# How the SwiGLU product is turned for the down projection: 128x128 squares on the matrix engine, or 32x32 squares and moves

## The chip, the cores and the metric

One core of a Trainium2 chip runs the whole program. The metric is the device time of one execution in microseconds (us). The core has the matrix engine PE (TensorE), the vector engine DVE, the scalar engine ACT, the engine POOL (GpSimd) and SP (SyncE), which here issues transfers. The engines are ordered among themselves by semaphores. 16 DMA engines carry the transfers.

## The reference, cut to what matters

```python
def swiglu(h, w_in, w_out):          # h: 256 x 2048, w_in: 2048 x 11264, w_out: 5632 x 2048, all float32
    gu = h @ w_in
    gate, up = gu[..., :D_FF], gu[..., D_FF:]
    return (jax.nn.silu(gate) * up) @ w_out

h = h + 0.5 * swiglu(rmsnorm(h, ffn1_norm), ffn1_w_in, ffn1_w_out)
# ... a pooling and gated-linear-attention mixer, and its output projection ...
h = h + 0.5 * swiglu(rmsnorm(h, ffn2_norm), ffn2_w_in, ffn2_w_out)
# ... then two attention layers (second_block), which the change doesn't touch
```

The sequence has 256 tokens, which lie on the partitions as 2 tiles of 128. The product silu(gate) * up has 5632 columns; these are the dimension that the second matmul sums over, so the product has to be turned before it can be an operand of it.

## The kernel before, in words

The kernel is a row of stages. A stage is n rounds; a round makes 512 output columns for both token tiles from 2048 rows of weights, which come in 8 chunks of 256 rows. Every float32 number is used as a sum of a rounded part (hi) and a rest (lo), so each product takes three matmuls: hi by hi, hi by lo, lo by hi (L1273 to L1275). A chunk is 2 row tiles by 2 token tiles by 3 matmuls, 12 matmuls of 128x512.

Each engine runs its own program over the same stages. A round of an ffn_in or ffn_out stage is as follows.

- **SP** (`load`) waits for each chunk c of round k until its place in `raw` is free, which is when chunk c of round k-1 has been split (`lo_done`), and issues two transfers for it. So SP is 8 chunks ahead of the split.
- **ACT** (`split_hi`, L1337) rounds a chunk into `whi`, and **DVE** (`split_lo`, L1522) subtracts to get `wlo`. There are 4 places for split chunks (`SPLIT`), so a chunk is split as soon as PE is through with the chunk 4 before it.
- **PE** multiplies the 8 chunks of the round.
- In the order of ACT and DVE a round k is: split chunks 4 to 7 of round k, turn what there is to turn (`batches_of`), split chunks 0 to 3 of round k+1 (`first_half`), and then `evacuate` round k. Chunk 3 of round k+1 can be split when PE has finished round k.

The two feed-forward networks have 3 ffn_in stages each, of 8, 8 and 6 rounds, each followed by an ffn_out stage of 4 rounds that uses what the ffn_in stage has made. An ffn_in round makes 256 columns of gate and the 256 matching columns of up. `evacuate` has ACT take silu of the gate half (L1390), and DVE multiply it by the up half into `hid[:, u]` (L1557; u is the parity of the round). That block of 256 tokens by 256 columns is then a batch `("hid", k)`: in the next round, between chunks 3 and 4, PE transposes it in 4 squares of 128x128 into a PSUM bank (`transposes`, L1231), ACT rounds the bank into the operand of the next stage (`operand_hi`, L1357), and DVE subtracts to get its rest (`operand_lo`, L1533). The block of an ffn_in stage's last round is a `Batch` of the ffn_out stage and is turned in its round 0. An ffn_out stage multiplies by block c in its chunk c; before each chunk of round 0 PE waits for the batch that makes the operand (`s.need[c]`).

First rounds are written out, the others are loops of two rounds (`paired_rounds`), whose waits count in registers. `tm` is a work area of 2 x 2048 numbers per partition that `hid` overlays.

Of the kernel before, what the change touches and what calls it, by code (L numbers as in the profile page):

```python
# [33 lines left out]
P = 128  # L34
# [5 lines left out]
NB = 512  # L40
HB = NB // 2
CH = 8
SPLIT = 4
# [83 lines left out]
def build(nc, A, out, upto=None):  # L127
    ctx = ExitStack()
    with ctx:
# [35 lines left out]
        h = sb("h", [P, TT, D])  # L165
        at = overlaid([("tm", [P, TT, D], F32)], [("hid", [P, 2, TT, HB], F32)])
        tm, hid = at["tm"], at["hid"]
        ab = overlaid([("bc", [P, 2, D], F32)],
# [91 lines left out]
        for n, s in enumerate(stages):  # L260
# [19 lines left out]
            if s.kind == "ffn_in" and nxt:  # L280

                s.hid_pair = nxt.pair
                nxt.before.setdefault(0, []).append(Batch(((s.n - 1) % 2,), nxt.pair, 2 * (s.n - 1)))
            if s.name in follows and nxt:
# [5 lines left out]

        n, latest = 0, {}
        for s in stages:
            for b in s.ahead:
                b.number, latest[b.pair, b.kt], n = n, n, n + 1
            for k in range(s.n):
                for c in range(CH):
                    if k == 0:
                        for b in s.mid.get(c, []):
                            b.number, latest[b.pair, b.kt], n = n, n, n + 1
                    if c == 4:  # L300
                        for b in s.before.get(k, []):
                            b.number, latest[b.pair, b.kt], n = n, n, n + 1
                        if s.kind == "ffn_in" and k:
                            if k == 1:
                                s.hid_batch0 = n
                            latest[s.hid_pair, 2 * (k - 1)], n = n, n + 1
                    if k == 0:
                        s.need[c] = latest[s.pair, s.chunk_tiles(c)[-1] // 2 * 2] + 1

        def batches_of(s, k, peeled):  # L310

            got = list(s.before.get(k, [])) if peeled else []
            if s.kind == "ffn_in" and not (peeled and k == 0):
                got.append(("hid", k))
            return got

        def resolve(s, b, u):

            if isinstance(b, Batch):
                return b.number, b.number % 2, b.pair, b.kt, b.gain  # L320
            k = b[1]
            return k - 1 + s.hid_batch0, (u - 1 + s.hid_batch0) % 2, s.hid_pair, (k - 1) * 2, None

# [84 lines left out]
        t_full, t_hi, t_done = sem("transposed"), sem("operand_hi_done"), sem("operand_done")  # L408
        silu_done = sem("silu_done")
        ident_in, const_in = sem("ident_in"), sem("const_in")  # L410


        LO0, USED0, FREE0 = CH, SPLIT, 2

# [717 lines left out]
        def _(sp):  # L1132
            xv = A["x"].rearrange("a (t p) n -> p (a t) n", p=P)
            for s in stages:
                w, k0, n0 = s.weights

                def load(k, u):
                    for c in range(CH):
# [10 lines left out]
                        for i in range(2):  # L1149
# [6 lines left out]
                            else:  # L1156
                                src = w[lo:lo + P, bass.ds(col + i * HB, HB)]
                                dst = raw[:, c, 0, i * HB:(i + 1) * HB]
                            sp.dma_start(dst, src).then_inc(landed[c], 16)

                paired_rounds(sp, s, load)
# [45 lines left out]
        def _(pe):  # L1207
            pe.sem_inc(chunk_used, USED0)

            def transposes(s, b, u):  # L1210
                number, parity, pair, kt, gain = resolve(s, b, u)
                dst = bank[4 + parity]
                if isinstance(b, Batch):
                    issued[0] = number + 1
                if not isinstance(b, Batch) or number >= 2:

                    pe.wait_ge(t_done, number - 1)
                if emitted[4 + parity]:

                    pe.wait_ge(freed_s[4 + parity], emitted[4 + parity])  # L1220
                if isinstance(b, tuple):

                    pe.wait_ge(acc_free, s.a0 + b[1] + FREE0)
                    src = [hid[:, (u - 1) % 2, t, j * P:(j + 1) * P] for j in range(2) for t in range(TT)]
                elif isinstance(b.source, tuple):
                    pe.wait_ge(acc_free, s.a0 + FREE0)
                    src = [hid[:, b.source[0], t, j * P:(j + 1) * P] for j in range(2) for t in range(TT)]
                else:
                    src = b.source(kt)
                for n, piece in enumerate(src):  # L1230
                    ins = pe.transpose(dst[:, n * P:(n + 1) * P], piece, ident)  # L1231
                ins.then_inc(t_full, 1)
# [52 lines left out]
            for s in stages:  # L1285
# [4 lines left out]
                def round_(k, u):  # L1290
# [6 lines left out]
                    for c in range(CH):  # L1297
# [28 lines left out]
        def _(act):  # L1326
# [14 lines left out]
            def operand_hi(s, b, u):  # L1341
                number, parity, pair, kt, gain = resolve(s, b, u)
                act.wait_ge(t_full, number + 1)
# [113 lines left out]
            for n, s in enumerate(stages):  # L1457
                nxt = stages[n + 1] if n + 1 < len(stages) else None

                def second_half(k, u):  # L1460
# [45 lines left out]
        def _(dve):  # L1506
            dve.sem_inc(lo_done, LO0)
            dve.sem_inc(acc_free, FREE0)
            steps = sem("vector_step")
            stepped = [0]  # L1510
# [14 lines left out]
            def operand_lo(s, b, u):  # L1525
                number, parity, pair, kt, gain = resolve(s, b, u)
                dve.wait_ge(t_hi, number + 1)
# [115 lines left out]
            for n, s in enumerate(stages):  # L1643
# [4 lines left out]
                def round_(k, u):  # L1648
# [61 lines left out]
```

## Time and profile before

| | us |
|---|---|
| median of 3 runs | 2788.77 |
| lowest and highest | 2787.61, 2790.61 |
| the profiled execution, its own time | 2788.64 |
| its span, first to last instruction | 2786.8 |
| PE busy | 2750.0 (99%) |
| DVE busy | 1495.4 (54%) |
| ACT busy | 1289.3 (46%) |
| DMA queue q1, share of 16 engines | 57.3% |
| mean granted PE clock | 0.998 |

The span is what the profile's views divide up; the execution's own time is 1.84 us longer. "Busy" counts the time an instruction is at work. PE's matmuls overlap, so its busy time is not its work at peak. The chain of waits follows the work back from the last instruction to what released each step.

### The profile page before, as it was taken

The numbers are of one execution on the slowest core, as the hardware profiler recorded it, in microseconds if no ns is written. First come the engines' busy times: TensorE is split into PE (matmuls) and PEld (weight loads), VectorE is DVE, ScalarE is ACT, GpSimd is POOL, SyncE is SP. The second block draws the span as 40 slices with busy tenths as digits, with TensorE's granted clock in tenths as the row PEclk, the third lists the DMA queues.
The fourth block names the chain that finished last, engine by engine and source line by source line (L and its number), as shares of the span: only waits on it lengthen the run. The fifth ranks groups of instructions, "written<-read, shape, count | busy, mean of one in ns | idle before, by whom it ended". The sixth has DMA issues, their size and how long they took to land.

```text
span 2786.8 us, 34415 instructions
## 1 busy us (share of the span) xinstructions
PE 2750.0 (99%) x12534; PEld 2260.5 (81%) x12534; DVE 1495.4 (54%) x1705; ACT 1289.3 (46%) x1653; POOL 63.6 (2%) x72
## 2 busy tenths in 40 slices
PE   7999999999999999999999999999999999999998
PEld 6888888888888788888888888887888888777877
DVE  4555455554544455455455545558555576455566
ACT  5443444344544455443444344544554464554463
POOL 1000000000000000000000000020000000020000
PEclk9999999999999999999999999999999999999999
DMA  9666666665644465655665565654465565546663
GB/s 258 191 189 193 191 190 187 195 189 177 193 153 151 147 199 183 189 191 193 190 189 190 193 189 174 196 183 152 136 204 169 171 196 188 157 137 198 185 177 131
DMA packets 375511, 506.09 MB, mean 182 GB/s; under 512 B 36022, under 2 KB 228736, under 8 KB 374608
## 3 DMA queue, kind: packets, MB, share of 16 engines
q1 hardware_dynamic: 373376, 495.84, 57.3%
q0 software_dynamic: 1824, 8.37, 0.9%
q8 instruction: 85, 1.39, 0.2%
q14 instruction: 50, 0.41, 0.0%
q10 hardware_dynamic: 176, 0.07, 0.0%
HBM read 502.06 MB, written 2.10 MB: 181 GB/s over the span
## 4 chain that ended last, share of the span: by engine, by line
PE 95%; DVE 2%; POOL 1%; ACT 1%; DMA 1%; issue 0%; SPq 0%; ACTq 0%; DVEq 0%; POOLq 0%
PE bank L1273 30%; PE bank L1275 30%; PE bank L1274 30%; PE bank L1231 2%; DMA h<-in_x_dram 1%; DVE wlo L1522 1%; POOL rope_b L850 1%; PE bank L997 0%; PE bank L798 0%; PE bank L782 0%; PE bank L1014 0%; PE bank L1023 0%; ACT whi L1337 0%; DVE isc L907 0%; PE bank L489 0%
## 5 line engine op out<-in xcount | busy, mean ns | idle before, releaser
L1522 DVE TENSOR_TENSOR wlo<-raw,whi 128x1024 fp32r<-128x1024 f32 (+2 forms) x976 | 1154.3, 1187 | 1227.6 <-ACT whi L1337 1223.6
L1337 ACT CAST whi<-raw 128x1024 fp32r<-128x1024 f32 (+2 forms) x976 | 988.6, 1016 | 1369.1 <-PE bank L1275 1363.3
L1273 PE MATMUL bank<-whi,p_hi 128*128 128x512 f32 x2016 | 799.1, 396 | 2.7 <-DVE wlo L1522 2.7
L1275 PE MATMUL bank<-whi,p_lo 128*128 128x512 f32 x2016 | 786.9, 390 | 0.0
L1274 PE MATMUL bank<-wlo,p_hi 128*128 128x512 f32 x2016 | 786.7, 390 | 0.0
L1273 PE MATMUL bank<-whi,q_hi 128*128 128x512 f32 x1696 | 667.9, 394 | 1.6 <-DVE wlo L1522 1.6
L1275 PE MATMUL bank<-whi,q_lo 128*128 128x512 f32 x1696 | 661.1, 390 | 0.0
L1274 PE MATMUL bank<-wlo,q_hi 128*128 128x512 f32 x1696 | 660.4, 389 | 0.0
L1273 PEld LDWEIGHTS bank<-whi,p_hi 128*128 128x128 f32 x2016 | 379.8, 188 | 86.6 <-issue 10.0
L1274 PEld LDWEIGHTS bank<-wlo,p_hi 128*128 128x128 f32 x2016 | 379.8, 188 | 79.8 <-issue 3.1
L1275 PEld LDWEIGHTS bank<-whi,p_lo 128*128 128x128 f32 x2016 | 379.5, 188 | 80.2
L1273 PEld LDWEIGHTS bank<-whi,q_hi 128*128 128x128 f32 x1696 | 318.7, 188 | 68.4 <-issue 3.9
L1275 PEld LDWEIGHTS bank<-whi,q_lo 128*128 128x128 f32 x1696 | 318.4, 188 | 67.1
L1274 PEld LDWEIGHTS bank<-wlo,q_hi 128*128 128x128 f32 x1696 | 318.9, 188 | 64.3
L1231 PE MATMUL bank<-con,h 128*128 128x128 f32 x224 | 32.5, 284 | 13.1 <-DMA h<-in_x_dram 9.3
L1231 PEld LDWEIGHTS bank<-con,h 128*128 128x128 f32 x224 | 27.4, 146 | 19.4 <-issue 12.2
L1557 DVE SCALAR_TENSOR_TENSOR hid<-bank,small,sg 128x256 f32<-128x256 f32 x88 | 38.3, 476 | 4.1 <-ACT sg L1390 4.1
L1390 ACT ACTIVATE sg<-bank,small 128x256 f32<-128x256 f32 x88 | 36.7, 468 | 0.0
L1568 DVE SCALAR_TENSOR_TENSOR h<-bank,h 128x512 f32<-128x512 f32 x56 | 35.9, 682 | 0.0
L1373 ACT ACTIVATE sg<-h 128x512 f32<-128x512 f32 x32 | 19.9, 624 | 29.9 <-DVE h L1568 29.9
L1538 DVE SCALAR_TENSOR_TENSOR p_lo<-bank,vec,p_hi 128x256 fp32r<-128x256 f32 x40 | 16.9, 477 | 21.5 <-ACT p_hi L1361 21.3
L1361 ACT ACTIVATE p_hi<-bank,vec 128x256 fp32r<-128x256 f32 x40 | 16.1, 473 | 25.5 <-PE bank L1231 25.5
(260 smaller groups left out, 998.8 us busy)
## 6 DMA issues: line engine op xcount, KB each, us to landing
raw<-in_ffn_w_in_dram SPq DMA_DIRECT2D x704, 256.0 KB, 2.9
raw<-in_ffn_w_out_dram SPq DMA_DIRECT2D x320, 256.0 KB, 3.0
raw<-in_w_in_a_dram SPq DMA_DIRECT2D x192, 256.0 KB, 3.0
raw<-in_w_in_mix_dram SPq DMA_DIRECT2D x128, 256.0 KB, 3.1
raw<-in_w_ple_gate_dram SPq DMA_DIRECT2D x128, 256.0 KB, 3.6
raw<-in_w_in_b_dram SPq DMA_DIRECT2D x128, 256.0 KB, 3.1
raw<-in_w_out_mix_dram SPq DMA_DIRECT2D x64, 256.0 KB, 3.2
raw<-in_w_o_a_dram SPq DMA_DIRECT2D x64, 256.0 KB, 3.4
```

The costliest lines, as they stand in the source:

```text
L850: ins = eng.tensor_tensor(dst, x, f, ALU.mult)
L1231: ins = pe.transpose(dst[:, n * P:(n + 1) * P], piece, ident)
L1273: pe.matmul(o, xht, wh, start=(kt == t_first), stop=False)
L1274: pe.matmul(o, xht, wl, start=False, stop=False)
L1275: ins = pe.matmul(o, xlt, wh, start=False, stop=(kt == t_last))
L1337: act.copy(whi[:, c % SPLIT, 0:n, 0:w], raw[:, c, 0:n, 0:w]).then_inc(hi_done, 1)
L1373: ins = act.activation(sgw[:, t, :], h[:, t, blk * NB:(blk + 1) * NB], ACT.Square, accum_out=parts[:, t, blk:blk + 1])
L1390: ins = act.activation(sg[:, u, t, :], pair[t][:, 0:HB], ACT.Silu, scale=rstd[:, t:t + 1])
L1522: dve.tensor_tensor(wlo[:, c % SPLIT, 0:n, 0:w], raw[:, c, 0:n, 0:w], whi[:, c % SPLIT, 0:n, 0:w].bitcast(F32), ALU.subtract).then_inc(lo_ ...
L1538: ins = dve.scalar_tensor_tensor(lo_[:, kt + j, :], src[:, j * SEQ:(j + 1) * SEQ], vec[:, g:g + 1], hi_[:, kt + j, :].bitcast(F32), ALU.mu ...
L1557: ins = dve.scalar_tensor_tensor(hid[:, u, t, :], pair[t][:, HB:NB], rstd[:, t:t + 1], sg[:, u, t, :], ALU.mult, ALU.mult)
L1568: ins = dve.scalar_tensor_tensor(hb, pair[t][:, :], c, hb, ALU.mult, ALU.add)
```

## The change

In place of ACT and DVE waiting for PE's squares, each block takes another way. DVE, straight after it has written `hid[:, u]`, transposes it with two instructions that turn each 32x32 square in itself (`hidq`). SP then moves the squares to their places with 16 transfers from SBUF to SBUF, each of 32 partitions by 128 numbers (`hidf`). ACT rounds from `hidf` into the operand, and DVE subtracts. A block of round k is turned at the end of round k, moved by SP while it loads round k+2 (after chunk 3), and rounded and subtracted by ACT and DVE after the splits of chunks 4 to 7 of round k+1. The last block of each ffn_in stage is also turned by DVE but not moved; PE transposes it from `hid` in round 0 of ffn_out as before.

```diff
-        at = overlaid([("tm", [P, TT, D], F32)], [("hid", [P, 2, TT, HB], F32)])
+        at = overlaid([("tm", [P, TT, D], F32)], [("hid", [P, 2, TT, HB], F32), ("hidq", [P, 2, 4, 2, TT, QB], F32),
+                                               ("hidf", [P, 2, 4, 2, TT, QB], F32)])
...
         def batches_of(s, k, peeled):
-            got = list(s.before.get(k, [])) if peeled else []
-            if s.kind == "ffn_in" and not (peeled and k == 0):
-                got.append(("hid", k))
-            return got
+            return list(s.before.get(k, [])) if peeled else []
+
+        def hidden_behind(s, k, u, peeled, behind):
+            if s.kind == "ffn_in" and not (peeled and k < behind):
+                return s, k - behind, (u - behind) % 2
+            if s.kind == "ffn_out" and peeled and k < behind - 1:
+                return s.hid_of, s.hid_of.n - behind + k, (s.hid_of.n - behind + k) % 2
+            return None
+
+        def moved_by(s, k, u):
+            return 16 * 16 * (s.moved0[u] + 1) + 8 * 16 * (k - u)
...
         @block.sync
+            def move_hidden(s, k, u):
+                sp.wait_ge(hid_turned, s.turned0 + k + 1)
+                sp.wait_ge(hid_done, s.turned0 + k - 1 + HID0)
+                for q in range(4):
+                    for f in range(4):
+                        sp.dma_start(hidf[f * QB:(f + 1) * QB, u, q, :, :, :], hidq[q * QB:(q + 1) * QB, u, f, :, :, :]).then_inc(hid_moved[u], 16)
...
                             sp.dma_start(dst, src).then_inc(landed[c], 16)
+                        if c == 3:
+                            made = hidden_behind(s, k, u, isinstance(k, int), 2)
+                            if made:
+                                move_hidden(*made)
...
         @block.tensor
-                if isinstance(b, tuple):
-                    pe.wait_ge(acc_free, s.a0 + b[1] + FREE0)
-                    src = [hid[:, (u - 1) % 2, t, j * P:(j + 1) * P] for j in range(2) for t in range(TT)]
...
-                            pe.wait_ge(t_done, s.need[c])
+                            if s.kind == "ffn_out" and s.chunk_tiles(c)[-1] // 2 == s.hid_of.n - 1:
+                                pe.wait_ge(t_done, s.last_hid.number + 1)
+                            elif s.kind == "ffn_out":
+                                pe.wait_ge(hid_done, s.hid_of.turned0 + s.chunk_tiles(c)[-1] // 2 + 1 + HID0)
+                            else:
+                                pe.wait_ge(t_done, s.need[c])
...
         @block.scalar
+            def hidden_hi(s, k, u):
+                act.wait_ge(hid_moved[u], moved_by(s, k, u))
+                for j in range(2):
+                    ins = act.copy(pair_hi[s.hid_pair][:, k * 2 + j, :].rearrange("p (t q n) -> p t q n", t=TT, q=4),
+                                   hidf[:, u, :, j, :, :].rearrange("p q t n -> p t q n"))
+                ins.then_inc(hid_hi, 1)
...
                     for b in batches_of(s, k, peeled):
                         operand_hi(s, b, u)
+                    made = hidden_behind(s, k, u, peeled, 1)
+                    if made:
+                        hidden_hi(*made)
...
         @block.vector
+            def hidden_lo(s, k, u):
+                dve.wait_ge(hid_hi, s.hid0 + k + 1)
+                for j in range(2):
+                    hi_, lo_ = (pair[s.hid_pair][:, k * 2 + j, :].rearrange("p (t q n) -> p t q n", t=TT, q=4)
+                                for pair in (pair_hi, pair_lo))
+                    ins = dve.tensor_tensor(lo_, hidf[:, u, :, j, :, :].rearrange("p q t n -> p t q n"), hi_.bitcast(F32), ALU.subtract)
+                ins.then_inc(hid_done, 1)
...
                                                        sg[:, u, t, :], ALU.mult, ALU.mult)
                     ins.then_inc(acc_free, 1)
+                    dve.wait_ge(acc_free, at_ + FREE0)
+                    for t in range(TT):
+                        ins = dve.transpose(hidq[:, u, :, :, t, :].rearrange("p f j n -> p j f n"),
+                                            hid[:, u, t, :].rearrange("p (j f n) -> p j f n", j=2, f=4))
+                    ins.then_inc(hid_turned, 1)
...
                     for b in batches_of(s, k, peeled):
                         operand_lo(s, b, u)
+                        if s.kind == "ffn_out" and b is s.last_hid:
+                            dve.sem_inc(hid_done, 1)
+                    made = hidden_behind(s, k, u, peeled, 1)
+                    if made:
+                        hidden_lo(*made)
```

## Rows read from the trace of the kernel before

**Rows 1.** The page, its first part (engines) and fourth (chain, by engine).
```profile
PE 2750.0 (99%) x12534; PEld 2260.5 (81%) x12534; DVE 1495.4 (54%) x1705; ACT 1289.3 (46%) x1653; POOL 63.6 (2%) x72
...
PE 95%; DVE 2%; POOL 1%; ACT 1%; DMA 1%; issue 0%; SPq 0%; ACTq 0%; DVEq 0%; POOLq 0%
```

**Rows 2.** Groups with shapes apart, whole span; columns as on the page.
```profile
L1273 PE MATMUL bank<-whi,p_hi 128*128 128x512 f32 x2016 | 799.1, 396 | 2.7 <-DVE wlo L1522 2.7
...
L1231 PE MATMUL bank<-con,hid 128*128 128x128 f32 x176 | 26.3, 271 | 0.0
```

**Rows 3.** Chain in order of time, 346 to 350 us: start, us, what.
```profile
346.49 0.23 PE bank L1275
346.72 0.44 PE bank L1231 x4
347.15 0.23 PE bank L1273
```

**Rows 4.** Timeline of ACT, 336 to 371 us: start, us, what, idle before it.
```profile
336.88 0.83 ACT L1390 ACTIVATE sg<-bank,small 128x256 f32<-128x256 f32 x2
...
344.03 1.05 ACT L1337 CAST whi<-raw 128x1024 fp32r<-128x1024 f32 x1 [1.67 <-PE bank L1275]
346.75 1.05 ACT L1337 CAST whi<-raw 128x1024 fp32r<-128x1024 f32 x1 [1.67 <-PE bank L1275]
347.71 0.58 ACT L1357 CAST q_hi<-bank 128x512 f32 x1
349.96 1.05 ACT L1337 CAST whi<-raw 128x1024 fp32r<-128x1024 f32 x1 [1.67 <-PE bank L1275]
...
369.96 0.58 ACT L1357 CAST q_hi<-bank 128x512 f32 x1
```

**Rows 5.** Timeline of DVE, 337 to 341 us.
```profile
338.15 0.87 DVE L1557 SCALAR_TENSOR_TENSOR hid<-bank,small,sg 128x256 f32<-128x256 f32 x2
```

**Rows 6.** SP: timeline at 346 us, weight issues at 783 to 806 us, their landing.
```profile
346.51 0.93 SPq L1159 DMA_DIRECT2D raw<-in_ffn_w_in_dram  x2
...
L1159 SPq DMA_DIRECT2D raw<-in_w_in_mix_dram x22: 327/431/902, 783.4 to 805.9; - x22
...
raw<-in_w_in_mix_dram SPq DMA_DIRECT2D x10, 8.0 KB, 1.7
```

**Rows 7.** DMA: packets at 783 to 797 us, queue q1 there and on the page, window 305 to 350.
```profile
DMA packets 1513, 0.24 MB, mean 17 GB/s; under 512 B 1440, under 2 KB 1440, under 8 KB 1512
...
q1 hardware_dynamic: 1512, 0.23, 10.3%
...
q1 hardware_dynamic: 373376, 495.84, 57.3%
...
305.00:350.00 45.00, 45.00 (x204) 37.21 (x204) 22.49 (x23) 19.29 (x23) 0.00 (x0) 1.00 0.61 190
```

**Rows 8.** Start of ffn1_in0, timelines of DVE and PE, 54 to 60 us.
```profile
54.94 0.88 DVE L1557 SCALAR_TENSOR_TENSOR hid<-bank,small,sg 128x256 f32<-128x256 f32 x2 [2.06 <-ACT sg L1390]
...
57.62 4.62 DVE L1522 TENSOR_TENSOR wlo<-raw,whi 128x1024 fp32r<-128x1024 f32 x4
...
59.34 0.60 PE L1231 MATMUL bank<-con,hid 128*128 128x128 f32 x4
```

**Rows 9.** Start of ffn2_in0, timelines of DVE and ACT, 1101 to 1110 us.
```profile
1102.03 0.88 DVE L1557 SCALAR_TENSOR_TENSOR hid<-bank,small,sg 128x256 f32<-128x256 f32 x2 [2.06 <-ACT sg L1390]
...
1108.90 0.58 ACT L1357 CAST p_hi<-bank 128x512 fp32r<-128x512 f32 x1
```

**Rows 10.** Groups with shapes apart: prices by size.
```profile
L1522 DVE TENSOR_TENSOR wlo<-raw,whi 128x1024 fp32r<-128x1024 f32 x912 | 1116.8, 1229 | 1145.2 <-ACT whi L1337 1141.3
L1337 ACT CAST whi<-raw 128x1024 fp32r<-128x1024 f32 x912 | 955.2, 1050 | 1292.2 <-PE bank L1275 1288.1 <-DMA raw<-in_ffn_w_in_dram 2.5 <-PE bank L1270 0.8
...
L1522 DVE TENSOR_TENSOR wlo<-raw,whi 128x512 fp32r<-128x512 f32 x48 | 32.8, 689 | 63.0 <-ACT whi L1337 63.0
...
L1337 ACT CAST whi<-raw 128x512 fp32r<-128x512 f32 x48 | 29.5, 618 | 57.5 <-PE bank L1275 57.2
```

More of the change, by code:

```diff
@@ L41 @@
 HB = NB // 2
+QB = 32
 CH = 8
@@ L165, in build @@
         h = sb("h", [P, TT, D])
-        at = overlaid([("tm", [P, TT, D], F32)], [("hid", [P, 2, TT, HB], F32)])
-        tm, hid = at["tm"], at["hid"]
+        at = overlaid([("tm", [P, TT, D], F32)], [("hid", [P, 2, TT, HB], F32), ("hidq", [P, 2, 4, 2, TT, QB], F32),
+                                               ("hidf", [P, 2, 4, 2, TT, QB], F32)])
+        tm, hid, hidq, hidf = at["tm"], at["hid"], at["hidq"], at["hidf"]
         ab = overlaid([("bc", [P, 2, D], F32)],
@@ L280, in build @@
             if s.kind == "ffn_in" and nxt:
-                s.hid_pair = nxt.pair
-                nxt.before.setdefault(0, []).append(Batch(((s.n - 1) % 2,), nxt.pair, 2 * (s.n - 1)))
+                s.hid_pair, nxt.hid_of = nxt.pair, s
+                nxt.last_hid = Batch(lambda kt, u=(s.n - 1) % 2: [hid[:, u, t, j * P:(j + 1) * P] for j in range(2) for t in range(TT)],
+                                     nxt.pair, 2 * (s.n - 1))
+                nxt.before.setdefault(0, []).append(nxt.last_hid)
             if s.name in follows and nxt:
@@ L289, in build @@
                         Batch(columns(h), pair, 4 * k + 2 * j, GAIN[gain] if gain else None) for j in range(2))
-        n, latest = 0, {}
+        n, turns, hids, moves, latest = 0, 0, 0, [0, 0], {}
         for s in stages:
@@ L294, in build @@
                 b.number, latest[b.pair, b.kt], n = n, n, n + 1
+            if s.kind == "ffn_in":
+                s.turned0, s.hid0, s.moved0 = turns, hids, list(moves)
+                turns, hids = turns + s.n, hids + s.n - 1
+                moves = [moves[0] + s.n // 2, moves[1] + s.n // 2 - 1]
             for k in range(s.n):
@@ L302, in build @@
                             b.number, latest[b.pair, b.kt], n = n, n, n + 1
[L303 to L307, printed above, removed]
+                    if k == 0 and s.kind != "ffn_out":
                         s.need[c] = latest[s.pair, s.chunk_tiles(c)[-1] // 2 * 2] + 1
         def batches_of(s, k, peeled):
-            got = list(s.before.get(k, [])) if peeled else []
-            if s.kind == "ffn_in" and not (peeled and k == 0):
-                got.append(("hid", k))
-            return got
[L317 to L322, printed above, removed]
+            return list(s.before.get(k, [])) if peeled else []
[7 more added lines that the diff above has]
+            return 16 * 16 * (s.moved0[u] + 1) + 8 * 16 * (k - u)
         def acc(a, t):
@@ L409, in build @@
         silu_done = sem("silu_done")
+        hid_turned, hid_hi, hid_done = sem("hidden_turned"), sem("hidden_hi_done"), sem("hidden_done")
+        hid_moved = [sem(f"hidden_moved_{u}") for u in range(2)]
         ident_in, const_in = sem("ident_in"), sem("const_in")
-        LO0, USED0, FREE0 = CH, SPLIT, 2
+        LO0, USED0, FREE0, HID0 = CH, SPLIT, 2, 2
         def round_before(s, k):
@@ L1210, in transposes @@
             def transposes(s, b, u):
-                number, parity, pair, kt, gain = resolve(s, b, u)
+                number, parity, pair, kt, gain = b.number, b.number % 2, b.pair, b.kt, b.gain
                 dst = bank[4 + parity]
-                if isinstance(b, Batch):
-                    issued[0] = number + 1
-                if not isinstance(b, Batch) or number >= 2:
+                issued[0] = number + 1
+                if number >= 2:
                     pe.wait_ge(t_done, number - 1)
@@ L1220, in transposes @@
                     pe.wait_ge(freed_s[4 + parity], emitted[4 + parity])
-                if isinstance(b, tuple):
-                    pe.wait_ge(acc_free, s.a0 + b[1] + FREE0)
-                    src = [hid[:, (u - 1) % 2, t, j * P:(j + 1) * P] for j in range(2) for t in range(TT)]
[L1225 to L1230, printed above, removed]
+                for n, piece in enumerate(b.source(kt)):
                     ins = pe.transpose(dst[:, n * P:(n + 1) * P], piece, ident)
@@ L1341, in operand_hi @@
             def operand_hi(s, b, u):
-                number, parity, pair, kt, gain = resolve(s, b, u)
+                number, parity, pair, kt, gain = b.number, b.number % 2, b.pair, b.kt, b.gain
                 act.wait_ge(t_full, number + 1)
@@ L1508, in _ @@
             dve.sem_inc(acc_free, FREE0)
+            dve.sem_inc(hid_done, HID0)
             steps = sem("vector_step")
@@ L1525, in operand_lo @@
             def operand_lo(s, b, u):
-                number, parity, pair, kt, gain = resolve(s, b, u)
+                number, parity, pair, kt, gain = b.number, b.number % 2, b.pair, b.kt, b.gain
                 dve.wait_ge(t_hi, number + 1)
```

## The prediction

> **What bounds the kernel now.** I read the page's first part, then its chain: PE is busy 99% of the span and the chain that ended last is PE for 95% of it [rows 1]. Then I read the groups with shapes apart. The reader is to see that the matmuls wait for almost nothing: 2.7 us of idle time before one of the two large matmul groups, all of it on DVE's split weights, and none at all before the transposes of `hid` [rows 2]. ACT and DVE, on the other hand, do nothing for more than half of the time: ACT has 1.67 us free before each split, and it is PE that ends this wait [rows 4]. So time comes off only where PE has less to do, and anything that ACT, DVE, SP and the DMA engines get in exchange costs nothing as long as split weights are ready when PE comes to them.
>
> **What PE loses.** The six ffn_in stages have 8, 8, 6, 8, 8 and 6 rounds, 44 blocks, and 44 x 4 = 176 transposes, which the group confirms [rows 2]. The last block of each stage stays, so 38 batches of 4 transposes go. The price of a batch has three readings. The group gives a mean of 271 ns for one, but 26.3 us for 176, since they overlap [rows 2]; 4 of these are 0.60. The chain, which counts each step only until the next begins, gives 0.44 us for the four [rows 3]. And the cadence of ACT, which here is set by PE, shows what a batch does to PE's chunks: a split follows the one before it by 2.72 us (344.03 to 346.75), but by 3.21 us where the batch lies between (346.75 to 349.96), which is 0.49 more; and a round is 369.96 - 347.71 = 22.25 us, where 8 chunks of 2.72 would be 21.76, again 0.49 [rows 4]. What the cadence has above the chain, 0.05, I put down to a slower start of the matmuls behind the transposes. I take 0.48 us between the two and nearer to the cadence, as it is measured from end to end. 38 x 0.48 = 18.2 us; the ends are 38 x 0.44 = 16.7 and 38 x 0.49 = 18.6. The waits that go with the batches on PE (for `t_done`, `acc_free`) had no idle time, so they give nothing more.
>
> The Trainium skill prices such a transpose otherwise. TensorE: Matmul & The Clock Gate, section Part 4: PE-mode transpose, has about 390 ns in isolation and about 275 ns in a kernel for 128x128 in bf16. By that, 152 transposes would be an estimated 42 us; the trace agrees with the 275 as the length of one (271 ns) but not as its cost, since four overlap into 0.44.
>
> **What DVE gets.** 88 square transposes of 128x256, 2 per block. The trace has no such instruction. Subtracts of 1024 and 512 columns take 1229 and 689 ns [rows 10], so one of 256 would take 689 - 540/2 = 419; the multiply of 128x256 takes 476 with an advance of 0.40 when two follow each other [rows 5]. I take 0.42 each, 0.85 for both with the wait between; below it could be next to nothing, above as long as the 1024-column subtract, 1.23 each. `hidden_lo` is 2 x 0.42 for a removed 0.68 of 512 columns (the 512-column price above). The room is ample: 8 splits of 1.23 and these make some 12.5 us in a round of 22.
>
> **What ACT gets.** Two copies of 256 columns for one of 0.58 [rows 4]. Casts of 1024 and 512 columns take 1050 and 618 ns [rows 10], so 256 are about 400, 0.80 for both. The short runs of 32 numbers in their addresses could double that; 1.6 still fits in the 1.67 free before a split [rows 4].
>
> **What SP gets, and the new wait.** 38 x 16 = 608 transfers, and ahead of each 16 a wait for DVE's squares. Two weight transfers of 256 KB are issued in 0.93 us; transfers of 8 KB in the narrow stage are issued in 327 to 902 ns, median 431 [rows 6]. So the issue doesn't depend on the size, and 16 of them take 16 x 0.37 = 5.9 to 16 x 0.47 = 7.5 us; I take 7.5. An 8 KB transfer lands after 1.7 us [rows 6].
>
> Now the times, in the round of [rows 4] and [rows 5]. DVE has written `hid` at 338.15 + 0.87 = 339.0 and the squares at 339.9. SP has by then issued chunk 3 of its load and waits; it issues until 347.4, and the last move lands at 349.1, or a microsecond later if the weights ahead of it in the queue hold it. ACT comes to `hidden_hi` where L1357 is now, 347.7, and waits some 1.4 to 2.6 us. Behind ACT's wait stand the splits of the next round's chunks 0 to 3, behind them DVE's. PE needs the first of these when it starts the next round: four chunks after its batch place, 346.7 + 4 x 2.72 = 357.6. Split hi and lo take 1.05 + 1.23 = 2.3, the two copies 0.8, so the last move may land at 354.5 without PE noticing. That is 4 us or more to spare, and the lag is made up at 1.67 us per chunk. It would be gone if an issue took (354.5 - 1.7 - 339.9) / 16 = 0.81 us.
>
> Behind SP's wait stand the weight transfers of chunks 4 to 7 of the round after next. They are issued up to 7 us late. Their cover is a full round of 22 us, so 15 are left for a landing that takes 1.7 us at 8 KB, and ACT doesn't wait for them. The moves don't pass POOL's queue.
>
> The DMA engines are 0.61 busy in such a round [rows 7]. A block adds 16 x 32 packets of 512 B, and from 10 transfers of 128 rows making 1440 packets I read 16 more per transfer for the semaphore: 768. At 15 ns each (10.3% of 16 engines for 14 us, over 1512 packets) this is 0.7 us per engine, at 68 ns (57.3% of the span over 373376) it is 3.3 [rows 7]. The share becomes 0.64 to 0.76, so weights keep landing in time.
>
> The Trainium skill, DMA: Bandwidth & Descriptors, section Measured (HBM→SBUF, 128 partitions, SWDGE, issued from GpSimd), says that transfers under 64 KB are dominated by descriptors, and its section Anatomy of one DMA — SWDGE (gpsimd) path puts a fixed cost of about 2.0 us on each. If those 2.0 us were paid one after another, 16 moves would be an estimated 32 us and wouldn't fit in a round.
>
> **Two late starts.** In ffn1_in0 the first `hid` is late, at 55.8 us, since the first silu waited for the norm [rows 8]. DVE's split of chunk 4 of round 1, the first of the four in its row, ends at 58.8 now; with 0.85 us of squares ahead of it, 59.7, and PE wants it at 59.3 [rows 8]: 0.4 us lost. The move of that block: squares at 56.7, issued until 64.2, landed at 65.9 to 67.1; the bound there is 59.3 + 10.9 - 3.1 = 67.1. So nothing is lost, but with hardly any room, and up to 2 us could be. In ffn2_in0 `hid` is ready at 1102.9 and the squares at 1103.8, landed at 1113.0; L1357 begins at 1108.9, which is 1.0 behind the batch place, so the bound is 1107.9 + 10.9 - 3.1 = 1115.7 [rows 9]: hidden. The other four stages start like the round above. The ffn_out stages lose nothing: block n-2 is done in ACT's and DVE's round n-1 of ffn_in, at least a whole round ahead of its chunk, and the last block goes as before.
>
> **Sum.** -18.2 + 0.4 = -17.8. The profiled execution's span of 2786.8 becomes 2769.0, its own time of 2788.64 becomes 2770.8, and the median, 0.13 above that, 2771.0. Its own range, from the ends of the terms: 16.7 - 2.4 = 14.3 to 18.6, 2770 to 2774.5, and 1 us each side for the runs.
>
> **Rivals.**
>
> *Moves land late (slower).* The place is ACT's wait in `hidden_hi`; it decides from 0.81 us per issue. For it speaks that SP does have issues of 0.90 us among the small transfers [rows 6]. At 0.90 each plus a gap of 0.04, 16 take 15.0 us, 2.1 beyond the 12.9 that there is, in each of 38 blocks: +80 - 18 = +62, about 2851. Against it: the median is 0.43, and only few are that long. Were moves served one after another at 1.7 us each, they would take 27.2 us where 14.6 are there: 38 x 12.6 - 18 = +461, about 3250. Against that speaks that two weight transfers are issued within 0.93 us, less than the landing of even an 8 KB one [rows 6]. 6% for both.
>
> *The gain is eaten, no change.* This takes 12 us or more back: 0.32 us per block, from matmuls that run slower beside the SBUF traffic, from a stall of 2 us in each of the first rounds (6 x 2 = 12), or because the squares take DVE far longer than any row suggests. 2777 to 2787, say 2783. Every stage would have to start as late as ffn1_in0, and four of the six don't. 6%. A smaller loss of 3 to 10 us by the same ways, 2775 to 2782: 12%.
>
> *PE's transposes cost their full length.* 152 x 0.271 = 41.2 us, 2747. Against it are the chain's 0.44 for four and the cadence. 2%. The Trainium skill's price named above would give the same.
>
> *The change doesn't take the work off PE*, if PE waits in ffn_out for `hid_done` as long as it saved. All blocks but the last are done before, so 1%, and it would be no change.
>
> *The forecast*, 2771: 73%.
>
> About 0.2% or 5.6 us is what a measurement of this kernel can tell from no change. Faster: 73 + 2 + nearly all of the 12, 87%. Same: 7%. Slower: 6%. The range goes from 2767 to 2781; most of what it leaves out is on the slow side.
>
> **What would show it.** In the changed profile L1231 on `hid` has 24 instructions; the cast behind the old batch place follows its predecessor by 2.72 us and not 3.21 unless ACT waits for the moves, and a round takes 21.8 us. SP shows rows of 16 transfers in 6 to 7.5 us. ACT's wait for hidf's transfer is 1 to 3 us in each block. The square transposes take about 0.4 us. The idle time of L1273 behind DVE stays under 5 us; if it is tens of microseconds, the first rival holds. If the round shrinks by 0.44 or less, my price of the batch was too high.

## The result

| | before | after |
|---|---|---|
| median, us | 2789.69 (4 runs) | 2772.55 (4 runs) |
| lowest and highest | 2787.61, 2790.94 | 2770.90, 2772.59 |
| span of the profiled execution | 2786.8 | 2769.1 |

The ratio is 0.9935 with a 95% interval of 0.9921 to 0.9949: 17.1 us faster by the medians, 2771.0 was forecast. A second set of five runs, made beside experiment 2, gave 2773.18 and 0.9942 (0.9929 to 0.9956), 16.1 us faster than the kernel before beside it (2789.25).

The page after, first and fourth part. They answer to [rows 1].

```profile
PE 2731.3 (99%) x12382; PEld 2244.7 (81%) x12382; DVE 1527.7 (55%) x1831; ACT 1290.0 (47%) x1691; POOL 63.6 (2%) x72
...
PE 95%; DVE 2%; ACT 1%; POOL 1%; DMA 1%; SPq 1%; issue 0%; ACTq 0%; DVEq 0%; POOLq 0%
```

PE is still 99% of the span and 95% of the chain. It has 152 instructions fewer (12382 for 12534), DVE has 126 more and ACT 38 more.

Groups with shapes apart, answering to [rows 2], and the source line of the moves with its landing time. Columns of the last two: instructions with shortest, median and longest duration in ns, and us to landing.

```profile
L1284 PE MATMUL bank<-whi,p_hi 128*128 128x512 f32 x2016 | 797.4, 396 | 4.0 <-DVE wlo L1550 4.0
...
L1242 PE MATMUL bank<-con,hid x24: 270/272/273, 213.7 to 1731.3; 128*128 128x128 f32 x24
...
L1149 SPq DMA_DIRECT2D hidf<-hidq x608: 507/590/1437, 56.7 to 1711.9; - x152
...
DMA to landing us min/median/max: 1.7/1.8/5.6
```

24 of the 176 transposes of `hid` are left, as forecast. PE's idle time behind DVE's split went from 2.7 to 4.0 us in this group. A move takes SP 590 ns to issue, and 16 come at one per 0.63 us, where I had 0.37 to 0.47 from weights.

Timeline of ACT after, two rounds, answering to [rows 4].

```profile
344.89 1.05 ACT L1353 CAST whi<-raw 128x1024 fp32r<-128x1024 f32 x1 [1.67 <-PE bank L1286]
349.35 0.71 ACT L1384 CAST q_hi<-hidf 128x256 f32 x2 [3.40 <-DMA hidf<-hidq]
349.97 2.00 ACT L1353 CAST whi<-raw 128x1024 fp32r<-128x1024 f32 x2
353.06 1.05 ACT L1353 CAST whi<-raw 128x1024 fp32r<-128x1024 f32 x1 [1.08 <-PE bank L1286]
...
366.65 1.05 ACT L1353 CAST whi<-raw 128x1024 fp32r<-128x1024 f32 x1 [1.67 <-PE bank L1286]
371.06 0.71 ACT L1384 CAST q_hi<-hidf 128x256 f32 x2 [3.35 <-DMA hidf<-hidq]
```

ACT stands still for 3.40 us until the last move has landed, then makes up for it: two casts run together, the next one still finds 1.08 us of idle time ended by PE. From one pair of copies to the next is 371.06 - 349.35 = 21.71 us; before, it was 22.25 [rows 4]. The next four rounds take 21.74 to 21.77, so the round lost 0.5 us, and PE never noticed ACT's wait.

Timeline of DVE and of SP in the same rounds, answering to [rows 5, 6].

```profile
358.00 0.87 DVE L1594 SCALAR_TENSOR_TENSOR hid<-bank,small,sg 128x256 f32<-128x256 f32 x2
358.91 0.77 DVE L1599 STREAM_TRANSPOSE hidq<-hid 128x256 f32<-128x256 f32 x2
```

```profile
338.00 10.04 SPq L1149 DMA_DIRECT2D hidf<-hidq  x16
348.28 10.94 SPq L1176 DMA_DIRECT2D raw<-in_ffn_w_in_dram  x16
359.71 10.04 SPq L1149 DMA_DIRECT2D hidf<-hidq  x16
```

The two square transposes take 0.77 us together. SP begins at once (359.71, the squares being there at 359.68) and needs 10.04 us for 16. The 16 moves and the 16 weight transfers of a round fill 10.04 + 10.94 of 21.7 us, which no step of the forecast had looked at.

### The profile page after: what moved, and what is told of

The parts are those of the page before. It is cut to its first block, busy times and chain, and to the rows that moved or that the text cites. A ratio compares the mean times of both kernels' runs of the same rounds, so it can differ in the third digit from the quotient of the medians.

```text
span 2769.1 us, 34994 instructions
## 1 busy us (share of the span) xinstructions
PE 2731.3 (99%) x12382; PEld 2244.7 (81%) x12382; DVE 1527.7 (55%) x1831; ACT 1290.0 (47%) x1691; POOL 63.6 (2%) x72
## 3 DMA queue, kind: packets, MB, share of 16 engines
q1 hardware_dynamic: 402560, 505.84, 58.3%
## 4 chain that ended last, share of the span: by engine, by line
PE 95%; DVE 2%; ACT 1%; POOL 1%; DMA 1%; SPq 1%; issue 0%; ACTq 0%; DVEq 0%; POOLq 0%
PE bank L1284 30%; PE bank L1286 30%; PE bank L1285 30%; PE bank L1242 1%; DMA h<-in_x_dram 1%; DVE wlo L1550 1%; POOL rope_b L858 1%; PE bank L1005 0%; PE bank L806 0%; ACT whi L1353 0%; PE bank L790 0%; PE bank L1022 0%; PE bank L1031 0%; SPq L1149 0%; DVE isc L915 0%
## 5 line engine op out<-in xcount | busy, mean ns | idle before, releaser
L1576 DVE TENSOR_TENSOR q_lo<-hidf,q_hi 128x256 f32 (+1 forms) x38 | 14.5, 422 | 64.7 <-ACT q_hi L1384 64.7
L1576 DVE TENSOR_TENSOR p_lo<-hidf,p_hi 128x256 f32 (+1 forms) x38 | 14.5, 422 | 62.7 <-ACT p_hi L1384 62.7
L1384 ACT CAST q_hi<-hidf 128x256 f32 (+1 forms) x38 | 13.6, 404 | 73.2 <-DMA hidf<-hidq 73.2
L1384 ACT CAST p_hi<-hidf 128x256 f32 (+1 forms) x38 | 13.6, 404 | 70.0 <-DMA hidf<-hidq 70.0
```

The source lines that it names most:

```text
L1384: ins = act.copy(pair_hi[s.hid_pair][:, k * 2 + j, :].rearrange("p (t q n) -> p t q n", t=TT, q=4), hidf[:, u, :, j, :, :].rearrange("p q ...
L1576: ins = dve.tensor_tensor(lo_, hidf[:, u, :, j, :, :].rearrange("p q t n -> p t q n"), hi_.bitcast(F32), ALU.subtract)
```

## What the clock adds to the comparison

Windows of 5 us at the three places where PE's clock was below full while it had work before, and, after, at its two and at one of the old ones. (The clock also falls in the last 5 us or so of each span, where PE has nothing left to do; that stretch is left out.) The columns are the window, its length, busy time and count of PE, weight loads, DVE, ACT and POOL, then granted clock, DMA share, GB/s.

```profile
26.00:31.00 5.00, 4.66 (x16) 3.94 (x17) 2.10 (x3) 1.77 (x3) 0.00 (x0) 0.66 1.09 359
842.00:847.00 5.00, 5.00 (x15) 4.03 (x16) 0.00 (x0) 2.94 (x6) 0.00 (x0) 0.66 0.28 100
2091.00:2096.00 5.00, 4.63 (x18) 4.09 (x19) 2.30 (x4) 1.17 (x2) 0.00 (x0) 0.66 0.34 105
```

```profile
28.00:33.00 5.00, 5.00 (x19) 3.89 (x19) 2.33 (x4) 2.00 (x4) 0.00 (x0) 0.69 1.09 359
842.00:847.00 5.00, 5.00 (x27) 4.17 (x26) 3.29 (x4) 2.83 (x5) 0.00 (x0) 1.00 0.57 188
2533.00:2538.00 5.00, 4.78 (x19) 4.22 (x20) 2.15 (x4) 1.17 (x2) 0.00 (x0) 0.66 0.35 105
```

A mean of 0.66 is some 3.4 us at the lower level of 1.2 GHz in a window otherwise at 2.4 GHz. At 842 us PE gets through 15 matmuls before and 27 after in the same 5 us, though not the same ones. By my estimate each such stretch costs what the clock fell short, 5 x 0.34 = 1.7 us. Three before and two after: 2786.8 - 5.1 = 2781.7 against 2769.1 - 3.4 = 2765.7, so by this count the change itself is worth 16.0 us of the 17.7 between the two spans. The same counting (the clock's shortfall, window by window) puts the second profile of the changed kernel at 2772.1 - 6.8 = 2765.3. Below, "at full clock" means a span reduced in this way. It rests on one profile of each kernel. The only measure of its error is that the two profiles of the changed kernel differ by 0.4 us, so a difference of that size isn't shown by it. It is used because the timed runs of one kernel lie further apart than that: of the changed kernel's four, three are within 0.06 us of each other and the fourth is 1.6 lower, about one such stretch.

## The experiments

**1. What four transposes cost PE.** All 44 hid batches of the kernel before, transposed twice over.

```diff
-                for n, piece in enumerate(src):
+                hidden = isinstance(b, tuple) or isinstance(b.source, tuple)
+                for n, piece in list(enumerate(src)) * (2 if hidden else 1):
```

> The kernel before, with each of its 44 hid batches transposed twice over (8 PE transposes into the same bank for 4; the second four write what the first four wrote). My theory: PE takes four further transposes at 0.44 us by the chain of waits, and the slower restart of the matmuls behind a batch, which was 0.05, doesn't double. So 44 x 0.44 = 19.4 us slower, 19 to 21. Rival, transposes cost their full length of 271 ns: 176 x 0.271 = 48 us slower. Rival, a batch costs mostly by its restart and its waits and little by the count of its transposes: under 10 us slower.

Measured: 2807.09 us, ratio 1.0063 (1.0046 to 1.0080), 16.8 us slower by the medians and 2800.8 - 2781.7 = 19.1 at full clock. The chain in order of time, one batch:

```profile
350.73 0.23 PE bank L1276
350.96 0.87 PE bank L1232 x8
351.83 0.23 PE bank L1274
```

Eight transposes pass in 0.87 us, twice the 0.44 of [rows 3]. Four cost 19.1 / 44 = 0.43 us, which is my 0.44, and the rival of 48 us falls. So does the figure of 275 ns that the Trainium skill gives for 128x128 in bf16 (TensorE: Matmul & The Clock Gate, Part 4: PE-mode transpose), taken as a price: it is a length.

**2. Is the new way hidden?** No moves, and ACT waits for the squares only.

```diff
-                        if c == 3:
-                            made = hidden_behind(s, k, u, isinstance(k, int), 2)
-                            if made:
-                                move_hidden(*made)
...
-                act.wait_ge(hid_moved[u], moved_by(s, k, u))
+                act.wait_ge(hid_turned, s.turned0 + k + 1)
```

(and `hidq` for `hidf` in what ACT and DVE read). This kernel leaves the squares where DVE wrote them, so it doesn't compute the same function.

> The changed kernel without any of the 608 moves and without ACT's wait for them: ACT waits for DVE's squares and makes the operand from the unmoved squares, so each feed-forward network works on wrongly placed numbers. My theory: the moves cost nothing except in ffn1_in0, where they make ACT 8.4 us late and PE about 1.8 us idle, so 1.5 to 2.2 us faster than the changed kernel, and PE's idle time behind DVE's split falls from 5.6 + 2.2 to about 6. Rival, the moves or ACT's wait of 3.4 us in each block cost PE a little every time (0.1 us or more per block): 6 us faster or more. Rival, the late start costs nothing and the forecast was off by the clock alone: no difference.

Beside it on the same chip, the changed kernel again:

> The changed kernel unaltered, so that the small differences of the runs beside it can be read on one chip. My theory: 16 to 18.5 us faster than before (38 x 0.48 = 18.2 less 2.0 at the start of ffn1_in0, where PE waits 0.2 and 1.6 us or a little more for split weights), a ratio of 0.9934 to 0.9943. It has no rival of its own; the other three are read against it.

Measured: 2769.41 us against 2773.18, 3.8 us by the medians, whose runs spread over 5.5 and 3.2 us; at full clock 2771.7 - 8.5 = 2763.2 against 2765.3: 2.1 us faster. The view of waits tells where they were (columns: who, for whom, us in total, times, longest). The changed kernel's second profile first, then the one without moves:

```profile
ACT q_hi L1384 <- DMA hidf<-hidq: 74.6, 19, 8.5
...
PE bank L1284 <- DVE wlo L1550: 5.7, 10, 1.3
...
PEld bank L1284 <- DVE wlo L1550: 2.3, 2, 1.7
```

```profile
PE bank L1280 <- DVE wlo L1546: 4.4, 9, 1.0
...
PEld bank L1280 <- DVE wlo L1546: 0.6, 1, 0.6
```

ACT waits for moves for 74.6 us in the 19 blocks of the first network and for 69.9 in those of the second, and all of it is worth 2.1 us at the end. The rival of 0.1 us per block would be 6 us or more faster. The loss is in ffn1_in0: PE and its weight loads wait for DVE's splits for 8.0 us in all against 5.0, and of these 5.2 against 2.2 lie between 40 and 75 us. The same place in the changed kernel's first profile, answering to [rows 8] (timelines of SP, ACT and DVE):

```profile
56.72 11.16 SPq L1149 DMA_DIRECT2D hidf<-hidq  x16
```

```profile
69.09 0.71 ACT L1384 CAST q_hi<-hidf 128x256 fp32r<-128x256 f32 x2 [8.39 <-DMA hidf<-hidq]
```

```profile
58.46 4.62 DVE L1550 TENSOR_TENSOR wlo<-raw,whi 128x1024 fp32r<-128x1024 f32 x4
```

16 moves took 11.16 us there, the last landed at 69.1, 8.39 us after ACT was ready for it, and my bound for it was 67.1. 69.1 - 67.1 = 2.0.

**3. Where does it stop being hidden?** 20, 24 and 32 moves per block; the ones beyond 16 write copies to an unused area.

```diff
-                for q in range(4):
-                    for f in range(4):
-                        sp.dma_start(hidf[f * QB:(f + 1) * QB, u, q, :, :, :], hidq[q * QB:(q + 1) * QB, u, f, :, :, :]).then_inc(hid_moved[u], 16)
+                for m in range(MOVES):
+                    q, f = m % 16 // 4, m % 4
+                    to = hidf if m < 16 else hidx
+                    sp.dma_start(to[f * QB:(f + 1) * QB, u, q, :, :, :], hidq[q * QB:(q + 1) * QB, u, f, :, :, :]).then_inc(hid_moved[u], 16)
```

> The changed kernel with 24 transfers per block for 16; the last 8 write copies of squares to an unused area and add to the same count that ACT waits for. My theory: a move is issued every 0.628 us (16 in 10.04), so 24 take 15.1 us. What PE can hide in a round, by the changed kernel's timeline: PE starts the next round at 366.6 + 10.9 = 377.4, of this 0.71 + 1.05 + 1.23 = 3.0 us are copies and the first split, so the last move may land at 374.4; the squares are there at 359.7 and the last landing takes 1.8, which leaves 12.9 us for the issues. So 15.1 is 2.2 too long, for 38 blocks: 82 us slower than the changed kernel, about 2852 to 2856, and the round takes 23.9 us. Rival, the wait is hidden anyway up to a full round (ACT and DVE catch up): within 5 us of the changed kernel. Rival, the wait for the moves already costs PE time in each block of the changed kernel: then 8 more moves cost their full 5.0 us per block, 190 us slower.

> The same with 32 transfers per block. My theory: 32 x 0.628 = 20.1 us of issues, 7.2 beyond the 12.9, 38 x 7.2 = 274 us slower than the changed kernel, about 3045, and a round of 28.9 us. If SP can't fit 32 moves and 16 weight transfers into that round (20.1 + 16 x 0.47 to 0.68 = 27.6 to 31 us), it is up to 350 slower. Rival, hidden up to a full round: under 30 slower. Rival, each further move costs in full: 38 x 16 x 0.628 = 382 us slower.

Measured: 24 moves 2912.53 us, ratio 1.0441 (1.0424 to 1.0459), 140 us slower than the changed kernel's 2772.55 for 82 expected; 32 moves, a single run, 3116.14, 344 slower for 274 expected. The first lies between my 82 and the rival's 190; for the second I had allowed up to 350 in case SP can't fit its issues into the round. I then tried a second model:

> The changed kernel with 20 transfers per block. 24 and 32 cost 140 and 344 us where I had 82 and 274, so I have a second model of the late case, a cycle. Once ACT is late by more than PE's lead, all four splits of the next round are done one after another ahead of the multiply that makes the next hid block, so from a landing to the next squares it takes 7.9 us (24 moves: ACT's copies at 358.89, squares at 366.80), then 0.65 us per move with its gap, then 1.3 to the copies. A round is 7.9 + 1.3 + 0.65 n: 25 for 24 moves (25.8 measured, 0.6 of it because SP was still at its weights), 30 for 32. For 20 it is 22.2, against PE's own 21.75: 0.45 x 38 = 17 us, so 10 to 25 us slower than the changed kernel, 2783 to 2798. The bound that I worked out first, 12.9 us of issues, is not reached by 20 x 0.628 = 12.6, and would have 0 to 3 us slower.

Measured: 2813.04 us, ratio 1.0081 (1.0064 to 1.0098), 40 us slower. Both models fall. The timelines of SP and DVE with 20 moves show what neither had:

```profile
360.81 10.22 SPq L1178 DMA_DIRECT2D raw<-in_ffn_w_in_dram  x16
371.20 10.06 SPq L1151 DMA_DIRECT2D hidf<-hidq  x16
381.30 2.49 SPq L1151 DMA_DIRECT2D hidx<-hidq  x4
384.06 9.68 SPq L1178 DMA_DIRECT2D raw<-in_ffn_w_in_dram  x16
```

```profile
369.04 0.78 DVE L1601 STREAM_TRANSPOSE hidq<-hid 128x256 f32<-128x256 f32 x2
```

The squares are there at 369.82, but SP is at its weight transfers until 371.03 and begins the moves at 371.20. It has no pause between: 384.06 - 360.81 = 23.25 us from one set of weights to the next, and ACT's copies are 385.10 - 361.88 = 23.22 apart. SP's own work is the round. 16 weight transfers issued without a pause take 9.3 to 10.4, a move 0.63, with some 0.4 between: 20 moves make 22.3 to 23.4, 24 make 25.6 (357.93 to 383.50 in that trace), 32 make 30.2 (464.34 to 494.52, ACT's copies 30.20 apart).

```profile
464.34 9.61 SPq L1178 DMA_DIRECT2D raw<-in_ffn_w_in_dram  x16
474.11 10.02 SPq L1151 DMA_DIRECT2D hidf<-hidq  x16
484.18 10.09 SPq L1151 DMA_DIRECT2D hidx<-hidq  x16
494.52 5.54 SPq L1178 DMA_DIRECT2D raw<-in_ffn_w_in_dram  x9
```

Over all rounds inside the stages that the traces show, ACT's copies are 22.8, 25.3 and 30.5 us apart in the mean, since the weight transfers vary; the round of 23.2 shown is one of the longer ones. For 38 blocks that is 40, 135 and 332 us above 21.75, and 40, 140 and 344 were measured. By the same count 16 moves make 9.8 + 10.04 + 0.4 = 20.2 of 21.75 us. SP is 93% full, and by my estimate two more moves would be as many as fit. I didn't take the rest of the load off SP with the number of moves kept, so that SP alone decides is read from the rows, not isolated by a run.

**4. Why a move takes 0.59 us.** Five series of 16 transfers behind the end of the kernel, each waited for before the next.

```diff
+                sp.dma_start(raw[32:64, c, i, 0:128], raw[0:32, c, i, 0:128]).then_inc(sem("shape_a"), 16)
...
+                sp.dma_start(raw[0:128, c, i, 0:512], win[0:128, n * 128:n * 128 + 512]).then_inc(sem("shape_e"), 16)
```

> The changed kernel with five series of 16 transfers added on SP behind the stored output, each series on a line of its own and waited for before the next: (a) SBUF to SBUF, 32 partitions x 512 B, other partitions; (b) SBUF to SBUF, 128 partitions x 512 B; (c) DRAM to SBUF, 32 x 512 B; (d) DRAM to SBUF, 128 x 512 B; (e) DRAM to SBUF, 128 x 2 KB. The question is why a move is issued every 0.628 us when weight transfers have 0.37 us of issue. My theory: it is the two SBUF ends, so (a) and (b) are at 0.51 to 0.59 us per issue, (c), (d) and (e) at 0.33 to 0.43. Rival, it is the small count of partitions: (a) and (c) slow, (b), (d), (e) fast. Rival, it is the load of the queue in the round: all five at 0.33 to 0.43. The time of the kernel itself means little here: some 50 us longer.

The source lines of the five, in that order:

```profile
L1196 SPq DMA_DIRECT2D raw<-raw x16: 512/590/592, 2770.0 to 2779.4; - x16
...
L1200 SPq DMA_DIRECT2D raw<-raw x16: 519/601/607, 2781.2 to 2790.8; - x16
...
L1204 SPq DMA_DIRECT2D raw<-in_w_in_mix_dram x16: 364/421/425, 2792.8 to 2799.7; - x16
...
L1208 SPq DMA_DIRECT2D raw<-in_w_in_mix_dram x16: 328/432/457, 2801.3 to 2808.6; - x16
...
L1212 SPq DMA_DIRECT2D raw<-in_w_in_mix_dram x16: 328/446/739, 2810.5 to 2818.3; - x16
```

The theory holds, at or a little above the ranges that I gave. With both ends in SBUF an issue takes 590 to 601 ns, from DRAM into SBUF 421 to 446, for 16 KB as for 64 or 256 KB, 32 partitions or 128. So for the issue what counts is the number of transfers and what they join, not what they carry.

**5. Fewer issues: through DRAM.** One transfer out, four back, with a semaphore `hid_out` and a DRAM buffer `away` of their own.

```diff
-                for q in range(4):
-                    for f in range(4):
-                        sp.dma_start(hidf[...], hidq[...]).then_inc(hid_moved[u], 16)
+                sp.dma_start(away[u], hidq[:, u, :, :, :, :].rearrange("p f j t n -> p f (j t n)")).then_inc(hid_out[u], 16)
+                sp.wait_ge(hid_out[u], 16 * (s.moved0[u] + 1) + 8 * (k - u))
+                for f in range(4):
+                    sp.dma_start(hidf[f * QB:(f + 1) * QB, u, :, :, :, :].rearrange("p q j t n -> p q (j t n)"),
+                                 away[u, :, f, :].rearrange("(q i) n -> i q n", q=4)).then_inc(hid_moved[u], 16)
```

> The changed kernel with another way to move the squares: one transfer of all 128 partitions from SBUF to DRAM, a wait for it on SP, and four transfers from DRAM to SBUF, each of 32 partitions by 4 squares: 5 issues for 16. My theory: a write of 256 KB lands after some 2.5 to 4 us, four loads are issued at 0.43 us and the last lands 1.8 us later, so the block is there 6 to 8 us behind DVE's squares, where it now takes 11.9. ACT comes to it 8 us behind the squares, so its wait falls from 3.4 us to under 0.5, in ffn1_in0 from 8.4 to about 3, and PE's 1.8 us of idle time there go. 1.5 to 2 us faster than the changed kernel, the same as without moves. Rival, a round trip through DRAM with a wait between takes longer than 11.9 us: ACT waits longer than now, no gain, and up to 3 us more at the start.

```profile
336.85 0.35 SPq L1149 DMA_DIRECT2D hidden_away<-hidq  x1
340.37 1.76 SPq L1152 DMA_DIRECT2D hidf<-hidden_away  x4
342.38 15.66 SPq L1180 DMA_DIRECT2D raw<-in_ffn_w_in_dram  x16
```

```profile
PE bank L1288 <- DVE wlo L1554: 4.4, 9, 1.0
...
ACT q_hi L1388 <- DMA hidf<-hidden_away: 1.8, 1, 1.8
```

SP's part ends 5.3 us after it began, and ACT's wait is 1.8 us once in place of 144.5 in 38 blocks. The time: median 2773.20 of runs from 2768.49 to 2773.60, ratio 0.9934 (0.9920 to 0.9948), the same as the changed kernel's 2773.18, and at full clock 2771.4 - 6.8 = 2764.6, 0.7 us faster where I had 1.5 to 2. That is too near to the 0.4 between two profiles of one kernel to be a gain shown. The waits for DVE's splits at the start are those of the kernel without moves (2.2 us between 40 and 75 us), so by them the 2.1 us should have come; whether they did stays open.

**6. The last block too.** First the edit in common: `last_hid` and its batch go, and `hidden_behind` serves one round more of ffn_out.

```diff
-            if s.kind == "ffn_out" and peeled and k < behind - 1:
+            if s.kind == "ffn_out" and peeled and k < behind:
```

Through DRAM:

> The kernel of the run before, and the last block of each ffn_in stage takes the same way (in round 0 of ffn_out) instead of PE's four transposes, so PE has no hid transposes left. My theory: six more batches at 0.48 us go from PE, 2.9 us. PE needs the last block in chunk 7 of ffn_out, and in chunk 6 in the two stages of 6 rounds, 6 x 2.72 = 16.3 us behind the start of the round; the squares are there 4 us behind it, plus 8 for the move and 1.6 for ACT and DVE, 13.6. So the gain is whole: 2.5 to 3.0 us faster than the run before, 4 to 5 us faster than the changed kernel, 2767 to 2769. Rival, the block is late in ffn_out: PE waits in chunk 6 or 7 and the gain is lost, seen as PE's wait for L1576's result.

Measured: 2770.30 us (2770.11 to 2771.33), ratio 0.9932 (0.9918 to 0.9945), at full clock 2768.4 - 6.8 = 2761.6: 3.0 us faster than through DRAM alone (2.9 forecast, and 2.9 by the medians), 3.7 faster than the changed kernel. It is the fastest version here that does the whole computation.

With the 16 moves from SBUF to SBUF:

> The changed kernel, with the last block of each ffn_in stage also moved by the 16 transfers from SBUF to SBUF, in round 0 of ffn_out. My theory: the block's squares are there 4.1 us after PE starts the round, the last of 16 moves lands 11.9 later, ACT and DVE take 1.6: 17.6 us. PE wants it in chunk 7 at 19.0 in the four stages of 8 rounds, and in chunk 6 at 16.3 in the two of 6. So PE waits about 1.3 us in two places, and of the 2.9 us that six batches are worth some 0.3 to 1 us is left. Rival, the wait doesn't matter: 2.9 us faster, as through DRAM. Rival, the block is late everywhere: slower than the changed kernel by 2 us or more, which would be the reason that PE keeps it.

Measured: 2781.61 us, ratio 0.9968 (0.9955 to 0.9980) where the changed kernel had 0.9942, and at full clock 2779.1 - 8.5 = 2770.6, 5.3 us slower than the changed kernel. The waits of PE:

```profile
PEld bank L1281 <- DVE p_lo L1571: 4.6, 1, 4.6
PE bank L1281 <- DVE p_lo L1571: 4.2, 1, 4.2
PEld bank L1281 <- DVE q_lo L1571: 3.6, 1, 3.6
PE bank L1281 <- DVE q_lo L1571: 3.2, 1, 3.2
```

PE's weight loads wait 4.6 and 3.6 us, once each, in the ffn_out stages behind the two stages of 6 rounds. I had 1.3 each, since I had taken chunk 6 to be 16.3 us behind the start. With 12 row tiles chunks 4 to 7 have only one each (`chunk_tiles`), so it is 4 x 2.72 + 2 x 1.36 = 13.6, and 17.6 - 13.6 = 4.0. -2.9 + 8.2 = +5.3 is what was measured at full clock, closer than this count is good for. The timed runs lose more, 0.0026 of 2790 or 7.3 us: the trace has one more stretch at a clock of 0.66, from 1740 to 1745 us, right behind the wait of 4.6, and the count at full clock leaves it out. Through DRAM the block needs 13.6 by my estimate, and PE's waits show none for it.

## Why the prediction was right, step by step

- **What bounds the kernel**: right. PE's share of the chain is 95% before and after, and only PE's work moved the time.
- **38 batches at 0.48 us, 18.2**: right. The loop's round fell from 22.25 to about 21.75; experiment 1 has 0.43 for four transposes added to a batch, and the six further batches of experiment 6 brought 3.0 us, 0.50 each. That the 0.05 to 0.07 between them is the restart of the matmuls behind a batch is argued, not shown.
- **DVE's squares at 0.42 each**: right, 426 ns median, 0.77 for two. ACT's copies 404 ns for 400, DVE's rest 422 for 419. Against these prices of plain rows the addresses in runs of 32 show no cost.
- **16 moves in 5.9 to 7.5 us**: wrong, 10.04. "The issue doesn't depend on the size" holds, but the rows were of transfers from DRAM, and the ends matter (experiment 4). ACT's wait became 3.4 us for 1.4 to 2.6, inside its cover.
- **Late start, 0.4 us lost, "up to 2 could be"**: mis-sized by the same term. It is 2.1 us, by experiment 2. With 11.2 us in place of 7.5 the block would have landed at 69.6, 2.5 behind its bound. The 0.4 was the squares' delay of DVE's split, which experiment 2 leaves in. Its price isn't isolated: PE's and its weight loads' waits for DVE's splits between 40 and 75 us are 0.4 us before and 2.2 without moves, but in the whole span only 4.2 and 5.0.
- **Sum**: -18.2 + 0.4 + 2.1 = -15.7; at full clock -16.0 was measured. That the two spans differ by 17.7, next to the -17.8 of the forecast, is 1.7 us of luck with the clock, which hid what the late start cost beyond the forecast.
- **The first rival's threshold, 0.81 us per issue**: wrong place. It is SP's own round that is full first, at about (21.75 - 10.2) / 16 = 0.72 us per move, or 18 moves of 0.63. The cover of SP's wait was reckoned for one round, as a delay that is made up; that a round's issues must also fit into the round was not reckoned at all.
- **The second half of that rival, moves one after another**: they overlap. One lands 1.8 us after its issue by the median, all 16 are there 11.3 us after SP begins (359.71 to ACT's copies at 371.06). The Trainium skill (DMA: Bandwidth & Descriptors, Anatomy of one DMA — SWDGE (gpsimd) path) gives a fixed cost of about 2.0 us for a transfer issued by GpSimd; these were issued by SP, and the 1.8 is near it as a latency. The 32 us that I had worked out for 16 in a row didn't come.
- **DMA share 0.64 to 0.76, weights in time**: queue q1 has 402560 packets for 373376, 48 more per move, as forecast. The weights of ffn_in land after 4.4 us for 2.9 by the page's median, and ACT waits for weights 1.8 us in the whole span, where it was 2.5 before. The window of [rows 7] shows 0.55 after, probably since SP's issues are no longer spread evenly, so it is not a test; 420 to 540 us has the share at 0.67, for 0.65 before, the low end of the forecast:

```profile
420.00:540.00 120.00, 120.00 (x533) 99.35 (x532) 63.68 (x68) 49.94 (x55) 0.00 (x0) 1.00 0.67 208
```

## What to carry to other kernels

Where one engine is the chain, its work is worth what it delays the instruction behind it (0.44 us for four overlapping transposes of 271 ns), and the cadence of the engines that follow it reads this off directly. What is moved off it must fit twice: its latency into the lead of whoever waits for it, and its issues into the round of the engine that issues them, next to what that engine has already. When the transfers are the cost, count them: by a detour with 5 of them a block was in place sooner than by 16 direct ones, though here the direct way was hidden too and the kernel's time didn't tell.

## What the runs showed of the hardware

A transfer from SBUF to SBUF took SP 590 to 601 ns to issue and one from DRAM to SBUF 421 to 446, at any size tried (experiment 4). Writing 256 KB to DRAM, waiting, and issuing four loads of 64 KB took 5.3 us, and the last load landed 1.9 us after its issue by the median; 16 direct moves were there after 11.3 us.

The granted clock was lower where PE had long waits in its rounds, and not wherever it waited. From 420 to 540 us PE was busy for 118.69 us with 20 moves, and the mean clock was 1.00; with 24 it was busy for 110.74, clock 0.99; with 32 for 92.68, clock 0.89, against 1.00 in the changed kernel, whose row stands above. PE had waited for DVE's split weights there, for at most 0.8, 3.4 and 7.9 us at a time.

```profile
420.00:540.00 120.00, 92.68 (x374) 74.76 (x373) 46.16 (x55) 36.76 (x48) 0.00 (x0) 0.89 0.51 157
```
